# The last projection's output gate multiplied into its weights, and its last quarter of columns in two pieces

## What is computed

```python
def hybrid_layer(x, c, norm_g, w_ada, b_ada, w_in, conv_w, w_o_attn, w_o_conv, w_out, rel_bias):
    mod = jax.nn.silu(c) @ w_ada + b_ada
    shift, scale, gate = jnp.split(mod, 3, axis=-1)
    h = rmsnorm_2(x, norm_g) * (1 + scale[:, None, :]) + shift[:, None, :]
    proj = h @ w_in
    ...
    y_attn = (attn * jax.nn.silu(g_attn)) @ w_o_attn
    y_conv = (short_conv(cb, cc, cx, conv_w) * jax.nn.silu(g_conv)) @ w_o_conv
    merged = jax.nn.sigmoid(m_attn) * y_attn + jax.nn.sigmoid(m_conv) * y_conv
    return x + gate[:, None, :] * (merged @ w_out)

def second_block(x, ...):
    x = hybrid_layer(x, ...)
    return rmsnorm_2(x, final_g)
```

## Time and profile before

| | us |
|---|---|
| median of 3 runs | 988.09 |
| the three runs | 985.48, 988.09, 988.38 |
| the profiled execution, its own time | 985.15 |
| its span, first to last instruction | 983.3 |

### The profile page before, as it was taken

One profiled execution on the slowest core, in us unless ns is written; L12 is line 12 of the kernel. 1 busy time (PEld: TensorE's weight loads), 2 busy tenths in 40 slices (PEclk: granted clock), 3 DMA queues, 4 the chain that ended last, 5 costly groups with the idle time before them and its releaser, 6 DMA issues.

```text
span 983.3 us, 14511 instructions
## 1 busy us (share of the span) xinstructions
PE 973.1 (99%) x6064; PEld 878.7 (89%) x6064; DVE 643.7 (65%) x807; ACT 508.1 (52%) x619; POOL 14.0 (1%) x12
## 2 busy tenths in 40 slices
PE   9999999999999999999999999999999999999997
PEld 8898888899999988988899999988999999988885
DVE  6898646676666658855776666658443777646473
ACT  7734465664444448556654444448434565444533
POOL 0000000000000000000000000000000000002000
PEclk9999999999999999999999999999999999999999
DMA  9953425467777674534467776764855544466611
GB/s 327 298 171 130 167 90 193 131 213 246 249 232 234 225 234 139 183 129 129 159 213 250 244 239 224 262 185 146 263 174 181 170 156 141 169 203 225 207 49 44
DMA packets 122869, 187.37 MB, mean 191 GB/s; under 512 B 5331, under 2 KB 88756, under 8 KB 122804
## 3 DMA queue, kind: packets, MB, share of 16 engines
q1 hardware_dynamic: 122368, 186.05, 57.4%
q10 hardware_dynamic: 436, 0.40, 0.1%
HBM read 185.37 MB, written 1.06 MB: 190 GB/s over the span
## 4 chain that ended last, share of the span: by engine, by line
PE 92%; DVE 4%; ACT 1%; DMA 1%; issue 1%; DVEq 0%; ACTq 0%
PE bank L611 90%; DVE wl L1092 1%; DMA raw<-in_ev_w_in 1%; DVE scr L1092 1%; ACT wh L1681 1%; PE bank L808 1%; PE bank L898 0%; DVE arena L1092 0%; ACT arena L1676 0%; PE bank L972 0%; DVE decay L1092 0%; DVE arena L1626 0%; DVE work L1349 0%; PE bank L768 0%; PE bank L674 0%
## 5 line engine op out<-in xcount | busy, mean ns | idle before, releaser
L1092 DVE TENSOR_TENSOR wl<-raw,wh 128x2048 fp32r<-128x2048 f32 (+1 forms) x157 | 356.7, 2275 | 204.7 <-ACT wh L1681 141.8
L1681 ACT CAST wh<-raw 128x2048 fp32r<-128x2048 f32 x155 | 294.0, 1907 | 177.8 <-PE bank L611 176.0
L611 PE MATMUL bank<-hh,wh 128*128 128x256 f32 x1088 | 308.5, 287 | 0.6 <-ACT arena L1830 0.5
L611 PE MATMUL bank<-hl,wh 128*128 128x256 f32 x1088 | 304.2, 283 | 0.0
L611 PE MATMUL bank<-hh,wl 128*128 128x256 f32 x1088 | 300.6, 283 | 0.0
L611 PEld LDWEIGHTS bank<-hh,wh 128*128 128x128 f32 x1088 | 207.8, 192 | 1.8 <-issue 1.4
L611 PEld LDWEIGHTS bank<-hl,wh 128*128 128x128 f32 x1088 | 207.8, 192 | 0.3
L611 PEld LDWEIGHTS bank<-hh,wl 128*128 128x128 f32 x1088 | 205.5, 192 | 0.0
L611 PE MATMUL bank<-wh,yh 128*128 128x512 f32 x416 | 162.7, 391 | 0.0
L611 PE MATMUL bank<-wl,yh 128*128 128x512 f32 x416 | 162.0, 389 | 0.0
L611 PE MATMUL bank<-wh,yl 128*128 128x512 f32 x416 | 161.9, 389 | 0.0
(11 more groups left out here) (190 smaller groups left out, 719.5 us busy)
## 6 DMA issues: line engine op xcount, KB each, us to landing
raw<-in_mlp_w SPq DMA_DIRECT2D x64, 1024.0 KB, 5.7
raw<-in_w_in SPq DMA_DIRECT2D x40, 1024.0 KB, 5.1
raw<-in_ev_w_in SPq DMA_DIRECT2D x19, 1024.0 KB, 5.3
raw<-in_w_ada SPq DMA_DIRECT2D x12, 1024.0 KB, 5.1
raw<-in_od_w_in SPq DMA_DIRECT2D x12, 1024.0 KB, 5.3
raw<-in_ev_w_out SPq DMA_DIRECT2D x6, 1024.0 KB, 4.8
raw<-in_od_w_out SPq DMA_DIRECT2D x4, 1024.0 KB, 4.8
raw<-in_w_o_conv SPq DMA_DIRECT2D x4, 1024.0 KB, 5.0
```

What stands on the lines that cost most here:

```text
L611: return eng.matmul(o, l, r, start=start, stop=stop, skip_group_check=True)
L1092: return eng.tensor_tensor(o, x, y, op)
L1681: eng.copy(part(wh, u), part(raw, u)).then_inc(S["hi"], 1)
```

## The change

Two edits go together.

First, the gate is multiplied into the rows of `w_out` instead of into the product. VectorE gets a function `gated_weights`, which multiplies a whole raw unit in place by `fin_gate`, once for each of the four `out6` units. It is called in iterations NU-9 to NU-6, for unit u+5, ahead of that iteration's splits. ScalarE's cast of these units and VectorE's subtract wait for a new semaphore, `gated`; the gate's DMA gets a semaphore of its own, `d_fgate`. In the tail each quarter's bank is then added to `x` directly.

Second, the last quarter (t = 1, columns 512 to 1023) is made in two pieces of 256 columns, each over all four units and in a bank of its own (`acc(1, 1)` and bank 2). VectorE adds the first piece and does the gain multiply for the other half while TensorE makes the second; ScalarE sums the squares of the pieces one after the other.

```diff
@@ VectorE
                 eng.wait_ge(S["hi"], SPLIT_OF[u] + 1)
                 wait_home(eng, u)
+                if u >= at("out6"):
+                    eng.wait_ge(S["gated"], u - at("out6") + 1)
                 tt(part(wl, u), part(raw, u), part(wh, u).bitcast(F32),
                    ALU.subtract).then_inc(S["lo_dve"], 1)
+
+            def gated_weights(u):
+
+                eng.wait_ge(raw_sem[u % RING], 16 * (u // RING + 1))
+                eng.wait_ge(S["d_fgate"], 16)
+                w = slot(raw, u)
+                tt(w, w, fin_gate.unsqueeze(1).broadcast_to([P, 2, D]), ALU.mult).then_inc(S["gated"], 1)
...
+                if NU - 9 <= u <= NU - 6:
+                    gated_weights(u + 5)
                 for s in splits_at(u)[u in GROUP_AT:]:
...
-                    wait_acc(eng, 6, t, half)
-                    link(tt(fin_p[:, t, c], acc(t, half)[:, :], fin_gate[:, c], ALU.mult))
-                    tt(x[:, t, c], x[:, t, c], fin_p[:, t, c], ALU.add).then_inc(S["fin_x"], 1)
-                tt(fin_p[:, t, half_of(0)], x[:, t, half_of(0)], fin_gain[:, half_of(0)], ALU.mult).then_inc(S["fin_g"], 1)
+                    if (t, half) != (1, 1):
+                        wait_acc(eng, 6, t, half)
+                        tt(x[:, t, c], x[:, t, c], acc(t, half)[:, :], ALU.add).then_inc(S["fin_x"], 1)
+                    else:
+                        eng.wait_ge(S["piece"], 1)
+                        tt(x[:, 1, end_columns(0)], x[:, 1, end_columns(0)], end_piece(0), ALU.add).then_inc(S["fin_x"], 1)
+                        gained(1)
+                        wait_used(eng, NU - 1)
+                        tt(x[:, 1, end_columns(1)], x[:, 1, end_columns(1)], end_piece(1), ALU.add).then_inc(S["fin_x"], 1)
+                if t == 0:
+                    gained(0)
@@ ScalarE
             def high(u):
                 eng.wait_ge(raw_sem[u % RING], 16 * (u // RING + 1))
                 wait_home(eng, u)
+                if u >= at("out6"):
+                    eng.wait_ge(S["gated"], u - at("out6") + 1)
                 eng.copy(part(wh, u), part(raw, u)).then_inc(S["hi"], 1)
...
+                if t == 0:
+                    act(sd[:, 10:11], st[:, 1:2], ACT.Sqrt, scale=1.0 / D, bias=st[:, 10:11]).then_inc(S["fin_sd"], 1)
+                else:
+                    act(st[:, 12:13], st[:, 3:4], ACT.Identity, scale=1.0 / D, bias=st[:, 11:12]).then_inc(S["fin_c"], 1)
+                    eng.wait_ge(S["fin_x"], 5)
+                    squares(fin_junk[:, 1, end_columns(1)], x[:, 1, end_columns(1)], 13, S["fin_ssq"])
+                    eng.wait_ge(S["fin_ssq"], 5)
+                    eng.wait_ge(S["fin_c"], 1)
+                    act(sd[:, 11:12], st[:, 13:14], ACT.Sqrt, scale=1.0 / D, bias=st[:, 12:13]).then_inc(S["fin_sd"], 1)
@@ TensorE, b_last
+                for piece in range(2):
+                    for u in range(first, NU):
+                        m = b_piece(u, piece, u == first, u == NU - 1)
+                        if piece == 1:
+                            m.then_inc(S["used"], 1)
+                    if piece == 0:
+                        m.then_inc(S["piece"], 1)
+
+            def b_piece(u, piece, first, last):
+                i, dst = UNITS[u][5], end_piece(piece)
+                for k in range(2):
+                    w_hi, w_lo = slot(wh, u)[:, k, end_columns(piece)], slot(wl, u)[:, k, end_columns(piece)]
+                    y_hi, y_lo = yh[:, 2 * i + k, P:2 * P], yl[:, 2 * i + k, P:2 * P]
+                    mm(dst, y_hi, w_hi, first and k == 0, False)
+                    mm(dst, y_hi, w_lo, False, False)
+                    m = mm(dst, y_lo, w_hi, False, last and k == 1)
+                return m
```

More of the change, by code:

```diff
@@ L318, in build @@
             "raw0 raw1 raw2 raw3 raw_half hi hi_half lo_half lo_dve used evac_act evac_dve "
-            "d_x0 d_x1 d_rows d_small d_tables d_causal d_wg d_u d_bias d_out d_grow d_gate "
+            "d_x0 d_x1 d_rows d_small d_tables d_causal d_wg d_u d_bias d_out d_grow d_gate piece fin_c d_fgate gated "
             "const d_masks masks cols colsT step_dve lo_ada mod x_ssq x_sd x_rs x_bc x_w x_n x_t hh hl hpart wk hturn "
@@ L450, in m_bank, with end_columns, end_piece @@
             return PS[(2, 3, 0, 1)[2 * t + half]]
+        def end_columns(piece):
+            return slice(512 + 256 * piece, 768 + 256 * piece)
+        def end_piece(piece):
+            return (acc(1, 1), PS[2])[piece][:, 0:256]
         def half_of(half):
@@ L579, in _ @@
                     eng.wait_ge(S["d_gate"], 16)
-                    eng.dma_start(fin_gate, gate_dram.broadcast_to([P, D])).then_inc(S["d_gain"], 16)
+                    eng.dma_start(fin_gate, gate_dram.broadcast_to([P, D])).then_inc(S["d_fgate"], 16)
                     eng.dma_start(fin_gain, a["final_gain"].broadcast_to([P, D])).then_inc(S["d_gain"], 16)
@@ L777, in b_last @@
                     for half in range(2):
+                        if (t, half) == (1, 1):
+                            continue
                         for u in range(first, NU):
@@ L782, in b_last @@
                             m = b_part(u, t, half, u == first, u == NU - 1)
[L783 to L786, removed]
+                        m.then_inc(S["acc"], 1)
                         if (t, half) == (0, 0):
                             merged_turn(1)
+                for piece in range(2):
[14 more added lines that the diff above has]
+                return m
             def spread(dst, col):
@@ L1655, in _, with gained @@
                         link(m)
-            eng.wait_ge(S["d_gain"], 32)
+            eng.wait_ge(S["d_gain"], 16)
+            def gained(t):
+                eng.wait_ge(S["fin_x"], 2 * t + 1)
+                tt(fin_p[:, t, half_of(0)], x[:, t, half_of(0)], fin_gain[:, half_of(0)], ALU.mult).then_inc(S["fin_g"], 1)
             for t in range(TT):
@@ L1996, in _ @@
                     eng.wait_ge(S["fin_x"], 2 * t + half + 1)
+                    if (t, half) == (1, 1):
+                        c = end_columns(0)
                     squares(fin_junk[:, t, c], x[:, t, c], 2 * t + half, S["fin_ssq"])
@@ L2003, in _ @@
                 eng.wait_ge(S["fin_b"], t + 1)
-                act(sd[:, 10 + t:11 + t], st[:, 2 * t + 1:2 * t + 2], ACT.Sqrt, scale=1.0 / D,
-                    bias=st[:, 10 + t:11 + t]).then_inc(S["fin_sd"], 1)
+                if t == 0:
[7 more added lines that the diff above has]
+                    act(sd[:, 11:12], st[:, 13:14], ACT.Sqrt, scale=1.0 / D, bias=st[:, 12:13]).then_inc(S["fin_sd"], 1)
                 eng.wait_ge(S["fin_g"], t + 1)
```

## The result

The change makes the kernel slower: 993.65 us median of 8 runs, against 987.47 for the kernel before in the same sessions, ratio 1.0058 with a 95% interval of 1.0043 to 1.0072. That is 5.7 us (4.2 to 7.1). The profiled execution took 993.35 us, its span is 991.5; before 985.15 and 983.3. The forecast was 991.4 us with a range of 987.8 to 994.3, so the median lies inside it, 2.2 us above the forecast.

A forecast was written before the change was run, and what follows sets the result against it. TensorE, busy for 99% and without a gap until 976.65, then a short VectorE and ScalarE chain set the end; +4.1 (stall) + 1.4 (clock) - 0.9 (tail) = +4.6 us on 986.8 gave 991.4 us, range 987.8 to 994.3.

The forecast's parts named there:

- Three of four multiplies are covered: VectorE before the output projection: multiplies of W0 to W2, 2.29 us each, fit gaps of 2.72, 3.58 and 2.72 us.
- The fourth is not, and costs a slot and a round trip: VectorE from 943.27: W3's multiply shifts merge(0) by 4.32 us, a 2.20 slot plus a 2.12 round trip to ScalarE.
- TensorE stalls by 4.1 us: TensorE at the eight transposes of the merged rows: resumes for good at 954.78 instead of 950.66, bounds 3.9 to 5.3.
- The clock falls and costs 1.4 us: TensorE during the stall: clock drops from 2.4 to 1.2 GHz, costing 1.4 us, bounds zero to 2.8.
- The tail gains 0.9 us: Last quarter and the chain behind the last matmul: -0.99 - 0.19 + 0.32 = -0.9 us, bounds -0.6 and -1.2.
- The row at 849: Trace row of 256-column matmuls starting every 0.12 us, used to price the last quarter's 48 matmuls at +0.32 us.
- Nothing waits next: Behind the transposes: the split of the turned rows keeps its 1.1 us of slack, so no second wait arises.
- Rival (a): Stall at the transposes without the clock's fall, TensorE at full clock: +3.2 us, 990.0 on the middle; chance 0.33.
- Rival (b): Not slower: W3's multiply is hidden, merge(0) shifts by less than 1.1 us; at best -0.9, 985.9; chance 0.09.
- (c): Low clock lasts into the rest of the projection, 10 us of it: +8.2 us, 995; chance 0.08 together with (d).
- (d): Last quarter's small pieces cost TensorE more than 0.32, up to 5.4 us more; chance 0.08 together with (c).
- two heights that nothing tells apart: Executions shown before the change: 985.15 and 985.48, 988.09 and 988.38 us; the forecast was set on their middle, 986.8.

The follow-up runs named there:

- The third experiment: The changed kernel with the fourth unit's multiply one place earlier in VectorE's program, ahead of the third unit's subtract; stretch 31.1 us, ratio 1.0016 to the kernel before.
- the fifth's busy wait: The changed kernel with seven unused dummy products on TensorE ahead of its wait for the merged rows (the busy stall); stretch 33.2 us, ratio 1.0035 to the kernel before.
- the fourth experiment: The changed kernel with the fourth multiply one place earlier and the second unit's subtract moved behind merged_low(0); stretch 29.0 us, ratio 0.9995 to the kernel before.

## Why the prediction held

The chain of reasons held link by link. Take 3.19 us (the shift) off the changed profile's times to compare with the prediction's.

- **Three of four multiplies are covered.** Right. The third starts at 939.24 (936.05), and ScalarE's cast of its unit at 941.85 (938.66), where it always was the earlier trace rows. The multiply takes 2.28 to 2.29 us with its broadcast operand, as the subtracts do.
- **The fourth is not, and costs a slot and a round trip.** Right, to the hundredth in places: multiply 943.27 as forecast, cast 945.66 (forecast 945.60), subtracts 947.66 and 949.87 (947.60, 949.80), merge(0) 952.07 (952.00). The third experiment separates the two: moved by one place, 2.1 us go.
- **TensorE stalls by 4.1 us.** 4.3 by the chains: the first 36 matmuls behind the transposes begin at 958.77 - 953.56 = 5.21 us into the stretch, before at 951.26 - 950.38 = 0.88. The second four start 4.49 us in, before 0.28, which is the 4.2 that the merge's shift explains but for 0.1 of handshakes; the last 0.1 is what four transposes by themselves take longer than in a row of eight.
- **The clock falls and costs 1.4 us.** It fell and cost 9.76 - 8.17 = 1.6 us. The mechanism was right and the timing in it was off: I took from the earlier trace rows that it falls 2.8 us after the last matmul; it fell 5.0 us after it, just when TensorE was back at work, and it was low for 3.4 us, not 2.8. That the price came out near is in part luck. By the prediction's own 2.8 us the clock would have fallen at 953.2, and of a low stretch of 2.8 us only some 1.2 would have lain behind 954.8, where the matmuls resume: a loss of 0.6 us, not 1.4. The later fall and the longer low stretch together made up for that, and no row had shown the length. The Trainium skill's page "TensorE: Matmul & The Clock Gate" (section "HAM oscillation") says that the burst behind a wait begins cold. Its case has waits of about 3 to 5 us, so with 3.1 us forecast it didn't make the low clock sure, as the prediction had it. The trace agrees with it: the fall came as the burst began, and its first eight matmuls ran slow, spaced by 0.43 instead of 0.227 us. The third experiment's gaps of 1.03 and 0.67 us, and the fifth's busy wait, didn't bring it on.
- **The tail gains 0.9 us.** 3.54 us behind the last matmul became 2.33, 1.21 less; the 96 matmuls take 0.34 more than the 72; net 0.87. The row at 849 was a fair price for the turned role: 0.12 us for each matmul of 256 columns. The figures of the Trainium skill (the same page, section "Back-to-back issue gap") would at 2.4 GHz have made that cost almost nothing; the traces show 0.31 to 0.34 us, so the rows were right.
- **Nothing waits next.** Right for the split of the turned rows, and the other quarters' adds.

The sum: +4.33 + 1.59 - 0.87 = +5.05 us, for +4.6 forecast. The terms that were somewhat short are the clock's and the stall's, 0.2 us each. The ratio's 5.7 us is 0.65 more than the profiles' difference, inside its interval; fastest against fastest (990.55 and 985.02) and slowest against slowest (995.27 and 989.85) give 5.5 and 5.4, and the rest isn't attributed. Of the 2.2 us between the forecast of 991.4 and the median, 0.7 is the starting point (986.8 taken, 987.47 measured over eight runs, which reach up to 989.85) and the rest the size of the loss.

Rival (a), the stall at full clock, needed the clock to survive; it did so only with TensorE's wait filled (33.2 us) or short. Rival (b), a hidden multiply, was wrong for this program order and is right for another: the fourth experiment is rival (b) made true. Its point was that merge(0) may slip by 1.1 us at most, and there it slips by 951.11 - 947.68 - 3.30 = 0.13. Rivals (c) and (d) didn't occur.

What the prediction left unexplained was the scatter of the executions shown, which it took as two heights that nothing tells apart. The first profile happened to be one without a low stretch in the middle of the kernel; the changed kernel's had two.

## What to carry to other kernels

Ahead of adding work to an engine that is mostly idle, look at the last stretch before its consumer: VectorE at 65% had room for three multiplies and none for the fourth, whose place lay in a run of instructions without a gap. An operation put between a load and a split shared by two engines costs its own slot and, if the other engine's step was running ahead, that round trip too, so place it beside something else and postpone what is needed later. A gap on TensorE is not priced by its length alone: read the granted clock behind it.

## What the runs showed of the hardware

TensorE's clock also fell where it had no gap at all. In the changed kernel's profile (windows, granted clock after the count):

```profile
395.00:396.00 1.00, 1.00 (x9) 0.66 1.06 412
396.00:397.00 1.00, 1.00 (x6) 0.50 0.88 338
...
398.00:399.00 1.00, 1.00 (x8) 0.64 0.32 31
423.00:424.00 1.00, 1.00 (x5) 0.50 1.02 422
```

TensorE reads busy throughout. What ran ahead of the first fall were sixteen f32 products with 8 columns, 3.5 us in one go (32 instructions in the trace); ahead of the second, four with 4 rows, 2.0 us, two 4x4 transposes and the score products:

```profile
390.80 3.64 PE L618 MATMUL bank<-wg,work 128*128 128x8 f32 x32
419.60 1.99 PE L618 MATMUL bank<-work,ident 4*128 4x256 f32 x8
```

Each fall lasted 3.4 us. By TensorE's chains the first shifted all later work by 1.5 us and the second by 1.6 (0.1 of the 3.2 us stands ahead of both), not by the 1.4 and 1.8 that an expectation above names. Two such falls make 3.1 us and don't reach from 985 to 990. In the profile of the kernel with the busy stall (993.36 us, its fastest execution 988.43) the first one lasted twice as long, 6.8 us, and began while the small products still ran:

```profile
392.00:394.00 2.00, 2.00 (x19) 0.95 1.05 402
394.00:400.00 6.00, 6.00 (x29) 0.50 0.58 202
400.00:402.00 2.00, 2.00 (x17) 0.85 1.00 369
```

It shifted what follows by 3.0 us, and the second place added 1.6. So the first place can cost nothing, 1.5 or 3.0 us and the second nothing or 1.6, which gives the four heights of the kernel before, about 985, 986.7, 988.4 and 989.9; none of its own executions at the three upper heights was profiled. Whether and how long the clock falls differs from one execution of the same kernel to the next. With the first group in two halves and the second in two pairs, full matmuls between, the clock stayed at 1.00 from 385 to 430 in the profile, and nine executions of nine stood within 0.5 us of each other. What decides it in one execution and not in the next, the runs don't show.
